# Weights split into high and low part: stored side by side and loaded with a step of two, the moving tile read from last token to first

## What is computed

```python
p = h @ w_in                                   # 1024 -> 28 units of 128 columns (a few narrower ones joined)
x = x + mixed @ w_out
x = x + (silu(gate) * up) @ w_down             # gate, up = split(causal_dwconv(h @ w_up) + b)
u = h @ conv_w_in; x = x + (gate_b * conv(gate_c * val)) @ conv_w_out
x = x + (silu(g) * u) @ w2                     # g, u = split(h @ w13), twice
ckv = hn @ w_dkv; kv = c_lat @ w_ukv; q = rms_norm(h @ w_dq) @ w_uq; x = x + attn @ w_o
```

## Time and profile before

| | |
|---|---|
| median of 2 runs | 1940.74 us (1940.49 to 1941.00) |
| profiled execution, first to last instruction (span) | 1938.3 us |
| PE busy | 1890.5 us (98%), 9271 matmuls, 9271 weight loads |
| PE weight loads busy | 1540.8 us (79%) |
| DVE, ACT, POOL busy | 959.2 us (49%), 739.5 us (38%), 237.1 us (12%) |
| DMA | 161 MB, mean 83 GB/s |

### The profile page before, as it was taken

The page is one execution under the profiler, slowest core; times in us unless marked ns, Lnnn a source line. Parts: engine busy times, 40 slices in busy tenths (PEclk is TensorE's granted clock), DMA queues, the critical chain, the costliest instruction groups (busy, mean ns, idle before and its releaser), DMA issues.

```text
span 1938.3 us, 25963 instructions
## 1 busy us (share of the span) xinstructions
PE 1890.5 (98%) x9271; PEld 1540.8 (79%) x9271; DVE 959.2 (49%) x1354; ACT 739.5 (38%) x1075; POOL 237.1 (12%) x196
## 2 busy tenths in 40 slices
PE   8989999999999999999999999999999999999998
PEld 6778867667888888888888888888776778888887
DVE  6464466654777763344454444333647444444322
ACT  6542543554444443232253333232455343333222
POOL 0051000102111111000021111101000121111100
PEclk9999998999999999999999999999999999999999
DMA  6310211113333333333333333333320133333332
GB/s 193 87 33 1 55 34 34 34 47 89 103 97 97 94 94 94 98 98 98 98 88 104 94 95 97 92 99 101 92 83 22 44 95 94 94 96 96 100 90 73
DMA packets 309223, 161.34 MB, mean 83 GB/s; under 512 B 12688, under 2 KB 306832, under 8 KB 309024
## 3 DMA queue, kind: packets, MB, share of 16 engines
q1 hardware_dynamic: 308080, 157.67, 28.1%
q0 software_dynamic: 640, 2.17, 0.3%
q10 hardware_dynamic: 432, 0.52, 0.1%
HBM read 158.24 MB, written 2.10 MB: 83 GB/s over the span
## 4 chain that ended last, share of the span: by engine, by line
PE 91%; DVE 4%; ACT 3%; issue 1%; POOL 0%; DMA 0%; ACTq 0%; DVEq 0%; POOLq 0%
PE ps L371 26%; PE ps L372 26%; PE ps L373 26%; PE ps L1063 1%; PE ps L1743 1%; PE ps L1491 1%; PE ps L1075 1%; PE ps L1501 1%; PE ps L2039 1%; PE ps L2040 1%; PE ps L1734 1%; PE ps L936 1%; ACT whi L358 1%; PE ps L920 1%; PE ps L1455 0%
## 5 line engine op out<-in xcount | busy, mean ns | idle before, releaser
L371 PE MATMUL ps<-xhi,whi 128*128 128x512 f32 x1656 | 656.6, 396 | 3.1 <-ACT ecol L989 2.1
L372 PE MATMUL ps<-xlo,whi 128*128 128x512 f32 x1656 | 647.7, 391 | 0.0
L373 PE MATMUL ps<-xhi,wlo 128*128 128x512 f32 x1656 | 647.6, 391 | 0.0
L358 ACT ACTIVATE whi<-raw 128x1024 fp32r<-128x1024 f32 (+2 forms) x297 | 309.0, 1040 | 707.6 <-PE ps L373 707.0
L366 DVE TENSOR_TENSOR wlo<-raw,whi 128x1024 fp32r<-128x1024 f32 (+2 forms) x297 | 365.8, 1232 | 278.6 <-ACT whi L358 278.6
L371 PEld LDWEIGHTS ps<-xhi,whi 128*128 128x128 f32 x1656 | 313.1, 189 | 72.1 <-issue 7.9
L373 PEld LDWEIGHTS ps<-xhi,wlo 128*128 128x128 f32 x1656 | 312.8, 189 | 65.9
L372 PEld LDWEIGHTS ps<-xlo,whi 128*128 128x128 f32 x1656 | 313.1, 189 | 65.3 <-issue 2.2
L621 DVE TENSOR_TENSOR zS<-ps,rs 128x512 f32<-128x512 f32 x132 | 91.3, 692 | 296.8 <-PE ps L373 284.6
L373 PE MATMUL ps<-h_hi,wlo 128*128 128x512 f32 x528 | 205.4, 389 | 0.0
L371 PE MATMUL ps<-h_hi,whi 128*128 128x512 f32 x528 | 205.4, 389 | 0.0
(11 more groups left out here) (339 smaller groups left out, 1718.7 us busy)
## 6 DMA issues: line engine op xcount, KB each, us to landing
raw<-in_conv_ffn_w SPq DMA_DIRECT2D x52, 512.0 KB, 3.8
raw<-in_mla_ffn_w SPq DMA_DIRECT2D x52, 512.0 KB, 3.8
raw<-in_w_up SPq DMA_DIRECT2D x44, 512.0 KB, 3.8
raw<-in_w_in SPq DMA_DIRECT2D x28, 512.0 KB, 3.8
raw<-in_conv_w_in SPq DMA_DIRECT2D x24, 512.0 KB, 3.7
raw<-in_w_down SPq DMA_DIRECT2D x16, 448.0 KB, 3.5
raw<-in_conv_ffn_w SPq DMA_DIRECT2D x16, 448.0 KB, 3.5
raw<-in_mla_ffn_w SPq DMA_DIRECT2D x16, 448.0 KB, 3.4
```

Of the source, the lines that this page charges most:

```text
L358: a.activation(whi[:, u % PARTS, 0:n], raw[:, u % RAW, 0:n], ACT.Copy).then_inc(hi_split, 1)
L371: t_.matmul(out, wh, xh, start=first, stop=False)
L372: t_.matmul(out, wh, xl, start=False, stop=False)
L373: return t_.matmul(out, wl, xh, start=False, stop=last)
```

## The change

Three things, and no instruction is added, removed or moved on any engine: the queues hold the same instructions in the same order. Only the addresses and steps of operands differ.

1. `whi` and `wlo` become `w_even` and `w_odd`, one buffer for each of the two slots. In it word 2n is the high part of the weight's word n and word 2n+1 its low part. ACT writes with a step of two words, DVE reads the high part and writes the low part with a step of two, and the weight load of a 128 x 128 slice takes every second word of 256.
2. In `product` the moving tile and the accumulator are both addressed from token 511 down to token 0, so each token's result lands where it did.
3. A gap of 64 words is put ahead of `w_even` and one of 32 words between the two buffers. Everything behind them moves up by 384 bytes.

The two units whose weight is the moving operand keep high and low part in separate halves of the buffer, and their passes are addressed as before.

```diff
-        whi = sb("whi", [P, PARTS, UNIT], F32R)
-        wlo = sb("wlo", [P, PARTS, UNIT], F32R)
+        sb("gap_even", [P, 64])
+        w_even = sb("w_even", [P, 2 * UNIT], F32R)
+        sb("gap_odd", [P, 32])
+        w_odd = sb("w_odd", [P, 2 * UNIT], F32R)
+        wsplit = [w_even, w_odd]
...
+        def is_moving(u):
+            return FIRST["ukv"] + 2 <= u < FIRST["uq"]
+
+        def split_part(u, low, n):
+
+            buf = wsplit[u % PARTS]
+            if is_moving(u):
+                return buf[:, UNIT * low:UNIT * low + n]
+            return buf[:, 0:2 * n].rearrange("p (n two) -> p n two", two=2)[:, :, low]
...
-            a.activation(whi[:, u % PARTS, 0:n], raw[:, u % RAW, 0:n], ACT.Copy).then_inc(hi_split, 1)
+            a.activation(split_part(u, 0, n), raw[:, u % RAW, 0:n], ACT.Copy).then_inc(hi_split, 1)
...
-            e.tensor_tensor(wlo[:, u % PARTS, 0:n], raw[:, u % RAW, 0:n], f32(whi[:, u % PARTS, 0:n]),
+            e.tensor_tensor(split_part(u, 1, n), raw[:, u % RAW, 0:n], f32(split_part(u, 0, n)),
                             ALU.subtract).then_inc(lo_split, 1)
...
-                wh, wl = (unit_view(b, u)[:, k, cols:cols + P] for b in (whi, wlo))
-                last = passes(acc(tile), wh, wl, x[0][:, k0 + k, :], x[1][:, k0 + k, :],
+                at = k * UNITS[u][2] + cols
+                wh, wl = (split_part(u, low, UNIT)[:, at:at + P] for low in range(2))
+                last = passes(acc(tile)[:, ::-1], wh, wl, x[0][:, k0 + k, ::-1], x[1][:, k0 + k, ::-1],
                               start and n == 0, stop and n == kt - 1)
```

More of the change, by code:

```diff
@@ L311, in full, with raw_view @@
             return ring(S.bank(key))
-        def unit_view(buf, u):
+        def raw_view(u):
             _, kt, n, _ = UNITS[u]
-            return buf[:, u % (RAW if buf is raw else PARTS), 0:kt * n].rearrange("p (k c) -> p k c", c=n)
+            return raw[:, u % RAW, 0:kt * n].rearrange("p (k c) -> p k c", c=n)
+        def is_moving(u):
[5 more added lines that the diff above has]
+            return buf[:, 0:2 * n].rearrange("p (n two) -> p n two", two=2)[:, :, low]
         def is_past(u, i, per):
@@ L329, in load_unit @@
             for r0, c0, m in pieces:
-                dst = unit_view(raw, u)[:, :, at:at + m]
+                dst = raw_view(u)[:, :, at:at + m]
                 src = A[name][r0:r0 + kt * P, c0:c0 + m].rearrange("(k p) c -> p k c", p=P)
@@ L343, in load_loop @@
                     src = A[name][r0:r0 + kt * P, bass.ds(col(i, j), n)].rearrange("(k p) c -> p k c", p=P)
-                    sp.dma_start(unit_view(raw, u), src).then_inc(unit_loaded[u % RAW], 16)
+                    sp.dma_start(raw_view(u), src).then_inc(unit_loaded[u % RAW], 16)
         def elements(u, i, per):
@@ L1998, in pe_mla @@
                 pe.wait_ge(lo_split, u + 2 + gr + 1)
-                wh, wl = (unit_view(b, u + 2 + gr) for b in (whi, wlo))
+                wh, wl = (split_part(u + 2 + gr, low, UNIT).rearrange("p (k c) -> p k c", k=2) for low in range(2))
                 for t in range(TT):
```

## The result

The changed kernel takes 1989.26 us (median of 2 runs, 1987.63 to 1990.88) against 1940.74: 1.026 times the time, 95% interval 1.0215 to 1.0304. It is slower by 48.5 us, where 70.6 us of gain were forecast. The profiled execution has a span of 1985.8 us (before 1938.3) at a mean granted clock of 0.986.

A forecast was written before the change was run, and what follows sets the result against it. PE was taken to bound the kernel: number of passes times their distance. 6537 passes x 10.8 ns = 70.6 us off the 1938.3 us span gave 1867.7, with 2.4 us around it 1870 us; range 1858 to 1942 us.

The forecast's parts named there:

- The count forecast to change, 6537: Passes expected to gain: 6948, less 48 whose weight is the moving tile, less 363 from 100 to 400 us.
- the surplus: At 2.4 GHz, each pass's 226.8 ns over the 213.3 ns its columns need: 13.5 ns, or 32 array cycles.
- two read streams meeting: Claimed origin of the 13.5 ns: weight load and moving tile, read at once, get in each other's way.
- keep their distance: Load and moving tile, at one speed and direction, either never meet in the same piece of memory or meet at every step.
- the good case: The two reads never meet in the same piece of memory: 10.8 ns gained a pass, 70.6 us in all.
- opposite directions make the meetings the same everywhere: In the kernel before, load and moving tile were taken to run oppositely, so buffer starts would not change the distance.
- The forecast distance, 216 ns: Time from one pass to the next at full clock after the change, down from 226.8 ns.
- The upper bound for what would be left of the surplus: At most 3 ns plus rounding over what a pass's columns take, after the change.
- Rival A: The load's cost goes by the lines it touches: 240 ns a pass, 88 us more, 2029 us; chance 0.17.
- Rival B: No change: cost follows words or loads, step and direction don't matter; 226.8 ns a pass, 1941 us; chance 0.14.
- Rival C: PSUM takes a descending accumulator at half rate: about 426 ns a pass, 1.3 ms more, 3.2 ms; chance 0.02.
- The splits: ACT and DVE splitting weights with a step of two: at most 1.0 us more each a unit, hidden; taken as nothing.

The follow-up runs named there:

- e3_no_gaps: The changed kernel without its two gaps: 1993.72 us, 1.0268 times the time of the kernel before.
- e6_gap64: The kernel before with one unused tile of 64 words ahead of `whi`, no other edit: 1938.74 us, 1.0001.
- e5_gap16: The kernel before with one unused tile of 16 words ahead of `whi`, no other edit: 1972.34 us, 1.0178.
- e8_gaps_only: The changed kernel's buffers and gaps, but high and low part in separate contiguous halves and tokens upward: 1962.14 us, 1.0120 times the kernel before.
- e1_reverse_only: The kernel before with only moving tile and accumulator of each product addressed from token 511 to 0: 1984.64 us, 1.0232.
- e4_sweep: A separate kernel computing none of the reference: groups of 32 equal matmuls, each group in one layout; contiguous and upward 226.9 ns a matmul.
- e12_types: Separate kernel of 32-matmul groups in three types, computing none of the reference: float32r 226.6 ns upward, 233.4 reversed; bfloat16 215.9; plain float32 429.2.
- e10_accumulator_reversed: The kernel before with only the accumulator written from token 511 to 0, so each product's tokens land reversed: 1938.91 us, 1.0000.

## Why the prediction was wrong

**What bounds the kernel, and the sum's form: right.** The time is the count of passes times their distance; 6784 x 6.9 ns is the 47 us that was lost. The count forecast to change, 6537, was close to those that did, 6784.

**That the surplus is two read streams meeting: supported, not shown.** Direction, step and distance between the two buffers change the matmul's pace, at 2.4 GHz and in float32r alone; the lower clock and the other types show nothing of it. No row shows a read being held up, and that equal addresses give two rhythms (e3_no_gaps) says that more than these addresses is at work. The Trainium skill ("TensorE: Matmul & The Clock Gate", Step-by-step, LDWEIGHTS) holds that the load has a read port of its own and takes no bandwidth from the running matmul. For bfloat16 (215.9 ns in each layout) the runs agree with it; for float32r they don't, since 16 unused words cost the whole kernel 1.8%.

**The step that failed** is that two streams at one speed and in one direction "keep their distance", of which I took the good case, 216 ns. Measured were 233.4 ns: 10.8 ns of gain a pass became 6.6 ns of loss. It rested on three supports, and each was weak.

- The reading of the earlier trace rows, that the surplus doesn't depend on where the buffers lie. The pairs in those rows have different names but the same phase (the start of one tile against the other, modulo 64 words): 64 words between `xhi` and `whi` change nothing (e6_gap64), 16 cost 6.6 ns (e5_gap16), and e8_gaps_only has `xhi` and `h_hi` good with opposite buffers once these are 32 words off. So in the kernel before all of them lie in step. Rows that agree because nothing varies in them were read as a test. From it followed "opposite directions make the meetings the same everywhere", and that the gaps are worth nothing; they cost 1.2% (e8_gaps_only).
- That the load is fetched from its last column to its first, so that a reversed tile would run along with it. No row showed the direction. The runs don't settle it either: upward is the better direction for a contiguous load in step (e1_reverse_only), and with a step of two both directions cost the same (e4_sweep). No group reads the stationary tile backward. What is shown is only that the reversal didn't help.
- That from two outcomes, "never meet" and "meet at every step", the good one would come. The text had no row for it, and still gave it 0.67.

**The forecast distance, 216 ns.** Nothing came under 226.6. The upper bound for what would be left of the surplus, 3 ns, had been taken from plain float32, and e12_types shows why that doesn't carry over: plain float32 has the same 2.5 ns in every layout, and none of the 13.3.

**Rival A** had the right sign and the wrong mechanism. It asked for 240 ns and 2029 us; 233.4 ns and 1989 us came. Beside a reversed tile a load with a step of two, which touches twice the memory, costs what a contiguous one costs (233.4 ns), and so does one of 32 columns. It decided from the first pass at the full clock on, as it said.

**Rival B** is refuted, and so is its rule that step and direction don't matter. **Rival C** is refuted by e10_accumulator_reversed: 1.0000. The Trainium skill ("Advanced Engine Details and Errata", PSUM Cachelines) says that output that isn't contiguous slows matmuls; a descending one, whose neighbours still lie together, doesn't.

**The splits: right.** ACT 0.12 us more a unit, DVE nothing, both inside the bound of 1.0 us and hidden behind 3.0 us of room; no wait of PE for a split has appeared.

**The range** ended at 1942 us, with 0.19 left for slower. The bounds in the text (213.3 to 240 ns) held the result. It was cut off by the chances, which rested on the step above.

**Open.** What the 13.3 ns in the best layout are; no layout tried removed them. Why the extra 6.7 ns needs more than 320 or 448 columns, and why equal starts that aren't multiples of 64 words cost up to 4 ns. What picks the rhythm of 233.3 or 236.7 ns. Which way the load is read. And whether the kernel without gaps is truly slower than the changed one.

## What to carry to other kernels

When float32r matmuls follow one another at the full clock, each with a load of its own, read both operands contiguously and upward, and keep their starts a multiple of 256 bytes apart; a small tile allocated between them cost 1.8% of this kernel. With 320 moving columns or fewer no such gain was measured. Before rows are taken as evidence that something doesn't matter, look whether it varies in them at all. And where a change alters how two streams meet, with no row of the altered case, give the bad meeting as much chance as the good one.

## What the runs showed of the hardware

- A float32r matmul of 512 columns with a load beside it takes 226.6 to 227.5 ns when both tiles start at a multiple of 64 words (256 bytes) in their buffers, however far apart (64 to 8000 words tried), and with the stationary tile 1, 3 or 4 words before that (2 words before: 233.1). Both moved alike, it takes 230 to 231 ns for 2 or 4 words and 227 to 228 for 8 to 48. Moved unlike, it takes 228.8 to 234.1 ns.
- With the moving tile read backward it takes 233.4 ns wherever the buffers start, 236.6 at three of sixteen starts. With the load stepping over words it takes 230 to 235.6 ns for steps of 2 to 4, and 245 to 248 ns for a step of 8.
- The same buffers can give 233.3 ns in one stretch and 236.7 in another (e3_no_gaps and the changed kernel): 48 and 56 array cycles over the columns, where the best layout has 32.
- A load of 128 float32 or float32r columns takes 111 to 112.5 ns at step one, 115 to 118 at step two and 227 to 233 at step four.
- A moving float32r tile of 512 columns read with a step of two words takes 14.66 / 32 = 458.1 ns (e4_sweep, L341, granted clock 0.84), and with a step of four 14.72 / 32 = 460.0 (L342, clock 1.00): twice the contiguous time, while the load alone takes the step of two nearly for nothing.
- Writing the accumulator backward costs nothing (1.0000, interval 0.999 to 1.0011).
- At the lower clock (426.7 ns), in bfloat16 (215.9 ns) and in plain float32 (429.2 ns) none of this shows.
